# A mixture-of-experts decoder kernel: rows fetched by selection matmuls inside the expert loop, and the up product split into parity and gate/up column groups

## The reference, cut to what matters

```python
D_MODEL = 1024; N_EXPERTS = 32; D_EXPERT = 256; TOPK_IN_GROUP = 2; DEPTH = 2

flat_e = expert_ids.reshape(m)              # m = 288 tokens x 2 experts = 576 slots
order = jnp.argsort(flat_e)                 # slots sorted by expert
rows = zeros(...).at[dest].set(xf[order // k])
hdn = jax.nn.silu(xb @ w_eg[e]) * (xb @ w_eu[e])   # gate and up product of a block of rows
out = hdn @ w_ed[e]                                # down product
y = einsum('nkd,nk->nd', y_slots, combine)         # weighted sum of a token's two experts
```

## Time and profile before

| | us |
|---|---|
| median of 3 runs | 1150.87 (1149.61 to 1157.13) |
| the profiled execution | 1153.77 |
| its span, first to last instruction | 1152.0 |
| PE busy in the span | 991.5 (86%) |
| PE weight loads / DVE / ACT / POOL busy | 636.3 / 386.1 / 465.6 / 83.7 |
| DMA | 319.03 MB, mean 277 GB/s |

### The profile page before, as it was taken

One profiled execution on the slowest core, in us unless ns is written; L12 is line 12 of the kernel. 1 busy time (PEld: TensorE's weight loads), 2 busy tenths in 40 slices (PEclk: granted clock), 3 DMA queues, 4 the chain that ended last, 5 costly groups with the idle time before them and its releaser, 6 DMA issues.

```text
span 1152.0 us, 22124 instructions
## 1 busy us (share of the span) xinstructions
PE 991.5 (86%) x7680; PEld 636.3 (55%) x7681; DVE 386.1 (34%) x1075; ACT 465.6 (40%) x825; POOL 83.7 (7%) x163
## 2 busy tenths in 40 slices
PE   4899999899799899777779999999996989977775
PEld 2567677477575444333356767747775534433333
DVE  1128622222441233222242582231327023322224
ACT  2325564300234455444443456441014445544443
POOL 1112000000300000000002200000012000000000
PEclk9889998989988899999989999898997999999998
DMA  9894324993553889999996332299630288999991
GB/s 384 306 397 146 110 75 137 423 420 140 195 206 115 357 352 421 422 422 421 422 419 226 140 117 73 88 354 419 259 113 35 85 360 339 423 422 421 422 422 67
DMA packets 65422, 319.03 MB, mean 277 GB/s; under 512 B 6051, under 2 KB 27875, under 8 KB 28227
## 3 DMA queue, kind: packets, MB, share of 16 engines
q1 hardware_dynamic: 63408, 315.06, 68.7%
q10 hardware_dynamic: 1810, 2.51, 0.6%
q0 software_dynamic: 128, 0.40, 0.1%
HBM read 315.44 MB, written 2.51 MB: 276 GB/s over the span
## 4 chain that ended last, share of the span: by engine, by line
PE 62%; DMA 20%; DVE 9%; ACT 5%; issue 3%; SPq 1%; POOLq 0%; POOL 0%; DVEq 0%; PEldq 0%; ACTq 0%
DMA ring<-wstream 20%; PE ps L566 19%; PE ps L1000 7%; PE ps L643 7%; PE ps L940 4%; PE ps L977 3%; PE ps L990 3%; PE ps L1009 3%; PE ps L599 3%; PE ps L980 2%; PE ps L817 2%; PE ps L709 1%; DVE work L1331 1%; ACT work L1164 1%; DVE top L1330 1%
## 5 line engine op out<-in xcount | busy, mean ns | idle before, releaser
L1000 PE MATMUL ps<-ring,work 128*32 128x512 f32 x976 | 123.0, 619 | 53.3 <-DMA ring<-wstream 51.7
L566 PE MATMUL ps<-h,ring 128*128 128x288 f32 x512 | 134.9, 418 | 0.7 <-ACT work L1094 0.7
L566 PE MATMUL ps<-work,ring 128*128 128x288 f32 x512 | 131.6, 416 | 2.9 <-DVE work L1421 2.9
L566 PEld LDWEIGHTS ps<-work,ring 128*128 128x128 f32 x512 | 97.8, 194 | 30.0 <-issue 3.7
L566 PEld LDWEIGHTS ps<-h,ring 128*128 128x128 f32 x512 | 97.4, 195 | 29.9 <-issue 4.1
L643 PE MATMUL ps<-h,ring 128*128 128x288 f32 x416 | 106.5, 417 | 8.7 <-ACT h L1108 6.3
L1220 ACT ACT_TABLE_LOAD x64 | 82.1, 1283 | 58.1 <-issue 58.1
L643 PEld LDWEIGHTS ps<-h,ring 128*128 128x128 f32 x416 | 80.4, 195 | 33.1 <-issue 10.9
L1220 ACT ACTIVATE work<-ps 128x512 f32<-128x512 f32 x64 | 38.2, 598 | 142.3 <-PE ps L1000 142.3
L1567 DVE SCALAR_TENSOR_TENSOR h<-work 128x288 f32<-128x288 f32 x128 | 60.6, 514 | 105.0 <-issue 105.0
L1000 PEld LDWEIGHTS ps<-ring,work 128*32 128x32 f32 x976 | 26.8, 112 | 122.5 <-issue 119.9
(11 more groups left out here) (251 smaller groups left out, 1111.4 us busy)
## 6 DMA issues: line engine op xcount, KB each, us to landing
ring<-wstream SPq DMA_DIRECT2D x280, 1024.0 KB, 17.2
work<-wstream SPq DMA_DIRECT2D x8, 1024.0 KB, 20.2
work<-pages SPq DMA_DIRECT2D x32, 192.0 KB, 3.5
work<-pages SPq DMA_DIRECT2D x32, 128.0 KB, 2.2
cs<-consts SPq DMA_DIRECT2D x1, 1218.0 KB, 8.3
x<-x_in SPq DMA_DIRECT2D x1, 1152.0 KB, 5.1
out_y<-h ACTq DMA_DIRECT2D x2, 576.0 KB, 2.8
out_vp<-v ACTq DMA_DIRECT2D x2, 256.0 KB, 3.3
```

The costliest lines, as they stand in the source:

```text
L566: last = mm(out, w[:, (k0 + k) * stride:(k0 + k) * stride + 128], rhs(k), start=(k == 0), stop=(k == n - 1))
L1000: last = mm(pgu[32 * c:32 * c + 32, :], xs[:, k, :], ws[k // 4][:, c * 512:(c + 1) * 512], start=(k < 4), stop=(k >= 4), skip_group_check= ...
```

## The change: what it does

The gather ahead of the expert stage is gone, and `xsort` with it. In its place each block's rows are fetched within the loop, one block ahead. POOL copies the block's 32 columns of `sel` to `sel_block`; PE multiplies them with `hrow` (`take_rows`: 12 matmuls of 256 columns in four column groups); ACT copies the 32 rows from PSUM (`keep_rows`); PE transposes them (`turn_rows`, 2 transposes); ACT copies them to `xs` (`stage_rows`). The first block's rows are fetched before the loop.

`up` now has 16 matmuls of 256 columns: a column group holds the sums of even or of odd feature chunks, for gate or for up. `fold_pairs` then adds only two parts, in 2 matmuls of 64 columns in place of 4 of 32. Their output shares a PSUM bank with the down product, so a wait on `y_kept` stands before them.

The table of blocks is made by POOL rather than DVE. DVE makes the second half of `sel` after the combining weights. `bc0` to `bc3` are computed straight from `dest` (3 matmuls each) without the detour through `rows4`. ACT loads the Silu table once before the loop. Six pairs are loaded apart (`EXTRA` = 6), seven experts are written out ahead of the loop (`EARLY` = 7), one after it.

```diff
@@ -135,9 +128,9 @@
     return dense + [(l, P_EXP + j) for j in range(3 * N_EXP) if j not in APART]
 
 
-EXTRA = 4
+EXTRA = 6
 APART = range(RING, RING + EXTRA)
-EARLY, ROUND = 6, RING // 3
+EARLY, ROUND = 7, RING // 3
 LATE = EARLY + (N_EXP - EARLY) // ROUND * ROUND
 STREAM = [entry for l in range(DEPTH) for entry in stream(l)]
 AT = {entry: i for i, entry in enumerate(STREAM)}
@@ -146,7 +139,7 @@
 SOFT = [5 if u[1] == 2 else 7 for u in UNITS]
 EXPS = [2 if u[1] == 2 else 4 for u in UNITS]
 IX = 68
-R_HOT, R_GAP, R_SEL0, R_SEL, R_WTS, ROUTE = 23, 24, 38, 45, 60, 64
+R_HOT, R_GAP, R_COUNTS, R_SEL0, R_WTS, R_SEL, R_COMB, ROUTE = 23, 24, 27, 38, 42, 49, 50, 53
 
...
+        squared = carve(6304, KD, T)
         drow = carve(4864, 4, T)
         slot = carve(4864 + 4 * T, N_EXP * MAXBLK)
         rt = [carve(4864 + i * 128, 128) for i in range(10)]
         hrow = carve(6304, 3, D)
-        xs = carve(6304, KD, BLK)
-        sg = carve(6560, 2, BLK)
-        hdn = carve(6624, 2, BLK)
-        gu = carve(6688, 512)
-        sel = carve(9376, 3, SLOTS)
-        extra = [carve(11200 + i * PAIR, PAIR) for i in range(EXTRA)]
+        xs = carve(2048, KD, BLK)
+        gu = carve(2304, 256)
+        xrow = v[:, 0, :]
+        sg, hdn = (v[:, 1, i * 2 * BLK:(i + 1) * 2 * BLK].rearrange("p (i s) -> p i s", i=2) for i in range(2))
...
                     of = first_projection[i - RING]
                     banks.wait_drained(sp, of, f"o{len(UNITS) - 1}")
-                    for j in range(EXTRA):
-                        sp.dma_start(extra[j], wstream[of * PAIRS + P_EXP + APART[j]]).then_inc(extra_w[j], 16)
+                    for j in range(EXTRA - 1):
+                        load_extra(of, j)
+                if i - RING in last_out:
+                    of = last_out[i - RING]
+                    banks.wait_full(sp, of, f"out{KD - 1}")
+                    load_extra(of, EXTRA - 1)
                 if i in pages1_at:
                     if i == RING:
...
+                    tabled.up(nc.gpsimd.tensor_scalar(more[:, n - 1], cnt[0:1, 0, :], n * BLK + 0.5, None, ALU.is_ge))
+                tabled.wait_so_far(g, l)
+                for n in (4, 2):
+                    step(tabled, nc.gpsimd.tensor_tensor(more[:, 0:n], more[:, 0:n], more[:, n:2 * n], ALU.add))
+                step(tabled, nc.gpsimd.tensor_tensor(more[:, 0], more[:, 0], more[:, 1], ALU.add))
+                step(tabled, nc.gpsimd.tensor_scalar(table[:, 1, 0:N_EXP], more[:, 0], 1.0, None, ALU.add))
+
+                route.wait(g, l, R_SEL)
+                g.wait_ge(rows_out, (l + 1) * (16 * 5))
                 hold(g, seen)
                 with g.Fori(0, N_EXP) as e:
                     first = g.value_load(table[0:1, 0, bass.ds(e, 1)], min_val=0, max_val=SLOTS)
...
-                        nc.gpsimd.tensor_copy(xs[:, :, :], xsort[:, :, bass.ds(at, BLK)]).then_inc(x_staged, 1)
-                        g.wait_ge(x_staged, n + 1)
+                        g.wait_ge(rows_taken, n + l + 1)
+                        nc.gpsimd.tensor_copy(sel_block, sel[0:TB, :, bass.ds(at, BLK)]).then_inc(sel_staged, 1)
+                        g.wait_ge(sel_staged, n + 1)
                         g.reg_add(seen, seen, 1)
-
...
@@ -923,29 +936,38 @@
                 if l + 1 < DEPTH:
                     next_modulation(range(NEXT_EARLY, KD))
 
-                for i, (k, hf) in enumerate(GATHERS):
-                    if i == ROWS_AT:
-                        ps = job("rows")
-                        route.wait(pe, l, R_WTS)
-                        for tb in range(3):
-                            last = nc.tensor.transpose(ps[0:4, tb * TB:(tb + 1) * TB], dest[0:TB, 7:11, tb], ident[0:TB, 0:TB])
-                        filled(last, "rows")
-                    if i == NEXT_AT and l + 1 < DEPTH:
-                        turn_modulation("next", "next_t")
-                    ps = job(f"x{k}.{hf}")
-                    if k == 0:
-                        route.wait(pe, l, (R_SEL0, R_SEL)[hf])
-                        banks.wait_drained(pe, l, "h5")
+                def take_rows(picks):
+
                     for tb in range(3):
-                        last = mm(ps[:, 0:T], hrow[0:TB, tb, k * 128:(k + 1) * 128], sel[0:TB, tb, hf * T:(hf + 1) * T],
-                                  start=(tb == 0), stop=(tb == 2))
-                    filled(last, f"x{k}.{hf}")
-
+                        for c in range(4):
+                            last = mm(px[32 * c:32 * c + 32, 0:256], picks[:, tb, :],
+                                      hrow[0:TB, tb, c * 256:(c + 1) * 256], start=(tb == 0), stop=(tb == 2), skip_group_check=True)
+                    last.then_inc(rows_taken, 1)
+
+                def turn_rows():
+
+                    for i in range(2):
+                        last = nc.tensor.transpose(px[:, 256 + i * 128:256 + (i + 1) * 128], xrow[:, i * 128:(i + 1) * 128], ident)
+                    last.then_inc(rows_turned, 1)
+
+                route.wait(pe, l, R_SEL0)
+                padded_x.wait(pe, l)
+                for n in TURNS:
+                    banks.wait_drained(pe, l, f"h{n}")
+                take_rows(sel[0:TB, :, 0:BLK])
+                hold(pe, seen)
+                pe.wait_ge(rows_kept, pe.snap(seen, min_val=0, max_val=200) + l + 1)
+                turn_rows()
+                if l + 1 < DEPTH:
+                    turn_modulation("next", "next_t")
                 for i in range(4):
                     ps = job(f"bc{i}")
                     if i == 0:
-                        route.wait(pe, l)
-                    filled(mm(ps[:, 0:T], cs[0:4, C_ONE:C_ONE + 128], rows4[0:4, i, :], start=True, stop=True), f"bc{i}")
+                        route.wait(pe, l, R_WTS)
+                    for tb in range(3):
+                        last = mm(ps[:, tb * TB:(tb + 1) * TB], bc(dest[0:TB, 7 + i, tb:tb + 1], [TB, 128]), ident[0:TB, 0:TB],
+                                  start=True, stop=True)
+                    filled(last, f"bc{i}")
 
...
@@ -994,37 +1016,53 @@
                 def up(ws):
 
                     n = pe.snap(seen, min_val=0, max_val=200)
-                    pe.wait_ge(x_staged, n + 1)
+                    pe.wait_ge(x_staged, n + l + 1)
                     for k in range(KD):
-                        c = k % 4
-                        last = mm(pgu[32 * c:32 * c + 32, :], xs[:, k, :], ws[k // 4][:, c * 512:(c + 1) * 512],
-                                  start=(k < 4), stop=(k >= 4), skip_group_check=True)
+                        for half in range(2):
+                            c = 2 * (k % 2) + half
+                            at = (k % 4) * 512 + half * D_EXP
+                            last = mm(pgu[32 * c:32 * c + 32, 0:D_EXP], xs[:, k, :], ws[k // 4][:, at:at + D_EXP],
+                                      start=(k < 2), stop=(k >= KD - 2), skip_group_check=True)
                     last.then_inc(gu_done, 1)
                     return n
 
-                def turn_and_combine(n):
+                def turn_and_combine(n, last_block=False):
 
                     pe.wait_ge(gu_kept, n + 1)
-                    for i in range(4):
-                        last = mm(pgut[:, i * BLK:(i + 1) * BLK], gu[:, i * 128:(i + 1) * 128], fold[:, :], start=True, stop=True)
+                    pe.wait_ge(y_kept, n + 1)
+                    for i in range(2):
+                        last = mm(pgt[:, :, i], gu[:, i * 128:(i + 1) * 128], fold_pairs[:, :], start=True, stop=True)
                     last.then_inc(gut_done, 1)
+                    pe.wait_ge(rows_kept, n + l + 2)
+                    if last_block:
+                        pe.sem_inc(rows_turned, 1)
+                    else:
+                        turn_rows()
                     combine(n)
                     pe.reg_add(seen, seen, 1)
 
-                def expert(e, next_blocks, rounds=0):
+                def take_next():
+
+                    pe.wait_ge(sel_staged, pe.snap(seen, min_val=0, max_val=200) + 2)
+                    take_rows(sel_block)
+
+                def expert(e, ahead, rounds=0):
 
                     ws = [expert_weight(e, i, rounds) for i in range(2)]
                     hold(pe, seen)
                     pe.reg_mov(blocks, blocks_ahead)
                     n = up(ws)
-                    pe.reg_mov(blocks_ahead, pe.value_load(next_blocks, min_val=1, max_val=MAXBLK))
+                    if ahead is not None:
+                        pe.reg_mov(blocks_ahead, pe.value_load(table[0:1, 1, ahead], min_val=1, max_val=MAXBLK))
                     if e:
                         down(n, e - 1, rounds)
                     else:
...
+                            take_next()
...
-                    turn_and_combine(pe.snap(seen, min_val=0, max_val=200))
-
-                ahead = pe.value_load(table[0:1, 1, 0:1], min_val=1, max_val=MAXBLK)
-                pe.reg_mov(blocks_ahead, ahead)
+                    if ahead is not None:
```

(59 more changed lines are left out.)

76 lines of the change are left out of this document (40 added, 36 removed).

## The result

The changed kernel took **1335.22 us** (median of 4 runs, 1329.58 to 1341.49), the kernel before 1152.12 us beside it: ratio 1.158 (95% interval 1.152 to 1.165). The forecast was 1175 us, with a range of 1138 to 1230. The direction was right, the size was not, and the time lies above the range: where the second rival stood, with its "over 1280 if all are lost".

What follows compares the result with a forecast made beforehand. The weight stream (DMA) bounded layer 0 from 460 us on, PE before; PE was to become the bound. Start and stage -18 us plus code holes +42 gave +24: profiled 1178, median 1175 us, range 1138 to 1230.

Steps and rivals of the forecast that it cites:

- the second rival: PE's loop no longer stays: one packet lost per pass +54 us, 1229; all lost, over 1280; chance 0.25.
- Start of the expert stage: Ahead of the first up product, replacing the gather: 20 us earlier in layer 0, 19 in layer 1, together -39 us.
- One block on PE: PE's time for one expert block in the loop: 7.3 us (7.0 to 8.0), where it was 5.75.
- The stage without holes: Expert stage: PE becomes the bound, 226.3 us plus 2 a layer, +20.8 over both; with the start -18 us.
- The code, straight-line part: Instruction packets up to the end of the loop's first pass: 18.7 packets arriving late, 21 us a layer, 42 in all.
- The code, the loop: The loop's later passes: the forecast, chance 0.48, had PE keep the loop without fetching it again, at no cost.
- sign for its own code term: In the profile: 69 instruction packets, "issue" idle and clock below 1 through the first 11 blocks, none later.
- sign for this rival: In the profile, for the loop no longer staying with PE: more than 69 packets, and packets in every pass.
- the packets did not keep up: Denies the first rival, packets keeping up in early blocks: 9.5 us a layer gives 1152, no holes 1133; chance 0.22.
- DMA did not bound the stage: Denies the third rival: blocks of 6.8 us or less, expert stage ending with the weight stream, -51 us, 1100; chance 0.05.

Runs made afterwards that it cites:

- the kernel whose loops stay: Changed kernel with 52 never-run matmuls ahead of layer 0's loop and 22 ahead of layer 1's, putting each on seven packets: 1191.93 us, ratio 1.033 to the kernel before.

## Why the prediction was wrong, by its own steps

**Start of the expert stage: right in layer 0, too large in layer 1.** The first up product was forecast at 336 and began at 335.51. The rows of what replaced the gather, timeline of PE, beside the earlier trace rows:

```profile
329.85 1.50 PE L943 MATMUL ps<-work 96*32 96x256 f32 x24 [0.65 <-DVE work L1578]
332.05 0.44 PE L950 MATMUL ps<-cs,v 128*128 128x128 f32 x2 [0.70 <-ACT v L1254]
332.33 0.60 PE L640 MATMUL ps<-cs,mraw 128*128 128x128 f32 x4
332.76 2.82 PE L968 MATMUL ps<-cs,dest 96*128 96x96 f32 x24
```

`take_rows` waited 0.65 us for DVE, which I had not foreseen, and then took 1.50 where 1.3 stood; `bc` took 2.82 where 3.1 stood. In layer 1 the first up was to be 19 us earlier after its layer's beginning and was 9.1. (The prediction's pieces for layer 1 add up to 888.6 and not 889.2, which changes nothing here.) Without the code for further blocks it was 17.8 (319.0 against 336.8). Of the 8.7 us between the two, 5.2 are the changed kernel's (324.2 against 319.0), and 4.3 of them lie at one hole of code, behind the last expert's part for further blocks and ahead of the mixer; the prediction had no such hole in this term:

```profile
644.56 0.77 PE L1034 MATMUL ps<-fold_pairs,work 128*128 128x64 f32 x4 [3.66 <-issue]
```

The other 3.5 us are the kernel before's, whose profiled execution without that code took that much longer there (336.8 against 333.3); why is open.

**One block on PE: right, 0.17 too dear.** 7.13 against 7.3, inside 7.0 to 8.0. `take_rows` was 0.2 under-priced, but the two transposes are one record each, not two (0.44 instead of 0.6), the fold takes 0.66 with its tail and leaves no idle time for the copy of the rows, where I had put 0.15, and the edges of the groups overlap.

**The stage without holes: right.** I had 226.3 and 2 for the first block; without the skipped code it is 222.2 and 223.8. PE was the bound, as said, and the slack in the late blocks was used up.

**The code, straight-line part: too small.** I took 21 us a layer, between 12 and 30. In the kernel whose loops stay, the stages take 34.4 and 28.4 us more than without the skipped code, and the whole kernel 67.7 more (1191.9 against 1124.2), where 42 stood. (In layer 0 this contains a hole at the 208 instructions put in for the move. The changed kernel itself, in its first eleven blocks, took 28.4 and 32.4 us more than without the skipped code, so the sum is nearly the same.) The count of packets fetched once was right within one, 68 where 69 stood. The price of one was not: I had 1.1 us, from a program in which some packets were late, and added a single allowance for the clock, while each hole here brings its own stretch at the lower level, 2.8 us after one of 4.5. That packets and not the work make these holes is seen from the kernel without skipped code, where a packet lasts PE 256/220 x 7.13 = 8.3 us and the blocks behind the first all took 7.2 us or less; at 5.3 us a packet (256/277 x 5.75; the prediction counted 271 instructions in place of 277 and had 5.4) there were holes, and at 4.2 (256/436 x 7.13) many.

**The code, the loop: this is the step that failed.** The likeliest case had the loop stay, at nothing. That was worth 143 us (1335.2 against 1191.9), more than all the other terms together. The prediction had the rival, wrote down that the loop lay "across 8" packets, and had the consequence of eight, a first packet pushed out, in its sentences on the Trainium skill. It then weighed this at 0.25, with no run against it: the kernel before, whose loop lay on five packets, says nothing of eight, and I let it count for the forecast. The rival's own price was wrong as well. It reckoned 5.4 us a lost packet and one loss a pass as the likelier size, 1229, and ended the range there. The loss is not of one packet: one miss leads to the next through the pass, nine packets and some 19 us each time (95.5 over five passes in layer 1). The prediction's sign for its own code term, no hole behind the first eleven blocks, failed with it, and its sign for this rival, packets in every pass, held in layer 1.

With the loop resident the forecast of 1175 would have met 1191.9, at the edge of its own range of 1157 to 1193. The other rivals: the packets did not keep up, and DMA did not bound the stage, as forecast.

**Still open.** Why a loop that reaches only 0.06 to 0.08 into its eighth packet is fetched again in some passes and not in others: the last packet may be left before the one behind it is asked for, but the traces show when a packet came and not which one it was.

## What to carry to other kernels

Count the instructions between a loop's start and its jump back, with the code that is jumped over, and the packets of 256 on which they lie: on seven it cost nothing after the first pass, on eight every pass could be fetched anew, and 88 idle instructions ahead of the loop decided it. Code that never runs costs at the rate at which it is passed: get it out of the path where the engine that passes it is the bound. A loop's behaviour in a smaller program is no evidence for a larger one until the size at which it changes is known; a rival whose cause can be counted should be counted out before it gets a chance.

## What the runs showed of the hardware that was not expected

- A loop one packet too long loses all of it: nine packets a pass, 48.4 us in place of 28.5.
- Packets arrived fast enough at one per 8.3 us of PE's work (no holes), not at one per 5.3 (some) or 4.2 (holes of up to 4.8 us in straight-line code, 6.3 at a jump back).
- After such a hole the granted clock was 0.50 for some 4 us: `take_rows` took 2.79 us instead of 1.50, combine's first part 2.09 instead of 1.15.
- An f32 transpose of 128x128 is one record, 0.44 us for two.
